# First step of an inference kernel rearranged: norm vectors transposed first, weight loads issued at once, first weight tile's products between the input transpositions

## The reference

```python
def rms_norm(x, g):
    xf = x.astype(jnp.float32)
    y = xf * lax.rsqrt(jnp.mean(xf * xf, axis=-1, keepdims=True) + EPS)
    return (y * g.astype(jnp.float32)).astype(x.dtype)

def half_step_ffn(x, g_pre, g_post, w_up, w_down):
    h = rms_norm(x, g_pre) @ w_up
    gate, up = h[..., :D_FF], h[..., D_FF:]
    y = (jax.nn.silu(gate) * up) @ w_down
    return x + 0.5 * rms_norm(y, g_post)
```

## Time and profile before

| | us |
|---|---|
| median of 3 runs | 1392.56 |
| lowest and highest | 1391.97, 1392.8 |
| span of the profiled execution, first to last instruction | 1389.6 |
| PE busy in it | 1266.4 (91%) |
| DVE, ACT, POOL busy | 936.1, 655.4, 290.0 |
| first weight product starts | 24.38 after the span's start |

### The profile page before, as it was taken

The page is one execution under the profiler, slowest core; times in us unless marked ns, Lnnn a source line. Parts: engine busy times, 40 slices in busy tenths (PEclk is TensorE's granted clock), DMA queues, the critical chain, the costliest instruction groups (busy, mean ns, idle before and its releaser), DMA issues.

```text
span 1389.6 us, 24055 instructions
## 1 busy us (share of the span) xinstructions
PE 1266.4 (91%) x9033; PEld 1202.5 (87%) x9033; DVE 936.1 (67%) x1555; ACT 655.4 (47%) x1100; POOL 290.0 (21%) x214
## 2 busy tenths in 40 slices
PE   5999999999367899999989999999966689999998
PEld 4999999889255899999989999987964479999998
DVE  3766644779996676664476665466999957766543
ACT  3544444444365654444455444454335475544432
POOL 3000000546461610000020000035564425000000
PEclk9999999999757999999999999999985599999998
DMA  5454555523200435454535455553340023545451
GB/s 173 141 184 159 164 173 164 161 92 125 87 0 1 161 122 181 151 165 156 165 119 184 154 171 164 164 190 122 106 138 1 0 70 123 173 160 180 144 167 58
DMA packets 179540, 184.63 MB, mean 133 GB/s; under 512 B 6627, under 2 KB 174827, under 8 KB 179470
## 3 DMA queue, kind: packets, MB, share of 16 engines
q1 hardware_dynamic: 178030, 181.93, 40.6%
q0 software_dynamic: 1056, 1.62, 0.5%
q10 hardware_dynamic: 384, 0.13, 0.0%
HBM read 179.73 MB, written 3.93 MB: 132 GB/s over the span
## 4 chain that ended last, share of the span: by engine, by line
PE 68%; DVE 25%; ACT 3%; issue 3%; DMA 0%; DVEq 0%; SPq 0%; ACTq 0%
PE ps L1110 21%; PE ps L1112 20%; PE ps L1111 20%; DVE yc L950 6%; DVE score L866 2%; DVE acc L736 2%; DVE m L864 2%; DVE x L757 2%; DVE hl L722 2%; DVE upd L749 1%; DVE prob L981 1%; DVE prob L969 1%; DVE ropb L839 1%; PE ps L1340 1%; DVE proj L843 1%
## 5 line engine op out<-in xcount | busy, mean ns | idle before, releaser
L1110 PE MATMUL ps<-hh,wlo 128*128 128x288 f32 x1920 | 575.8, 300 | 19.2 <-DVE hl L722 10.1
L1111 PE MATMUL ps<-hl,whi 128*128 128x288 f32 x1920 | 567.6, 296 | 0.0
L1112 PE MATMUL ps<-hh,whi 128*128 128x288 f32 x1920 | 565.8, 295 | 0.0
L712 DVE TENSOR_TENSOR wlo<-raw,whi 128x1024 fp32r<-128x1024 f32 (+1 forms) x269 | 320.5, 1193 | 287.0 <-ACT whi L403 283.7
L403 ACT ACTIVATE whi<-raw 128x1024 fp32r<-128x1024 f32 (+1 forms) x336 | 347.4, 1035 | 236.5 <-PE ps L1112 213.2
L1110 PEld LDWEIGHTS ps<-hh,wlo 128*128 128x128 f32 x1920 | 361.2, 188 | 27.5 <-issue 14.2
L1112 PEld LDWEIGHTS ps<-hh,whi 128*128 128x128 f32 x1920 | 362.7, 189 | 0.0
L1111 PEld LDWEIGHTS ps<-hl,whi 128*128 128x128 f32 x1920 | 361.9, 188 | 0.6
L1050 POOL TENSOR_TENSOR wlo<-raw,whi 128x1024 fp32r<-128x1024 f32 x67 | 166.3, 2499 | 492.1 <-ACT whi L403 492.0
L1110 PE MATMUL ps<-ghi,wlo 128*128 128x288 f32 x704 | 208.4, 296 | 0.0
L1111 PE MATMUL ps<-glo,whi 128*128 128x288 f32 x704 | 207.7, 295 | 0.0
(11 more groups left out here) (202 smaller groups left out, 1186.5 us busy)
## 6 DMA issues: line engine op xcount, KB each, us to landing
raw<-in_ffn_w_up SPq DMA_DIRECT2D x88, 1024.0 KB, 5.1
raw<-in_ffn_w_down SPq DMA_DIRECT2D x32, 1024.0 KB, 5.1
raw<-in_w_in SPq DMA_DIRECT2D x24, 1024.0 KB, 5.2
raw<-in_ffn_w_down SPq DMA_DIRECT2D x16, 768.0 KB, 4.5
raw<-in_w_out SPq DMA_DIRECT2D x8, 1024.0 KB, 5.1
kc<-in_cache_k SPq DMA_DIRECT2D x2, 1024.0 KB, 8.1
vc<-in_cache_v SPq DMA_DIRECT2D x2, 1024.0 KB, 8.3
xrow<-in_x_prompt SPq DMA_DIRECT2D x1, 1024.0 KB, 5.4
```

The costliest lines, as they stand in the source:

```text
L712: dve.tensor_tensor(wlo[:, split_slot, 0:n, :], raw[:, raw_slot, 0:n, cols], whi[:, split_slot, 0:n, :].bitcast(F32), ALU.subtract).then_i ...
L1110: pe.matmul(out, wlo[:, slot, k, :], hi, start=start, stop=False)
L1111: pe.matmul(out, whi[:, slot, k, :], lo, start=False, stop=False)
L1112: return pe.matmul(out, whi[:, slot, k, :], hi, start=False, stop=stop)
```

## The change

SP no longer waits for the identity before it issues the first two weight loads. PE waits for the identity and for the nine vector loads, transposes the vectors, and then waits for x. The first step of the first block has its own order, `very_first_step`: four slices of x are transposed; then, four times, the three products of tile 0 with slice k and the transpositions of slice k + 4; then tile 1 with slices 0 to 3, both tiles with slices 4 to 7, the taps' transpositions, and tiles 2 and 3, the sum of squares between them. ACT makes a whi after every second hh. DVE takes the copies and the low parts by turns, reads the low part's x from PSUM, and makes wlo of tiles 0, 2 and 3; POOL makes that of tile 1.

```diff
                     sp.dma_start(xrow[0:DEC, 2, :], ins["x_sample"][0]).then_inc(x_in, 16)
-                    sp.wait_ge(ident_in, 16)
                     sp.dma_start(raw[:, 0], strip_view("ffn1_w_up", 0, 0, D, 0)).then_inc(loaded[0], 16)
...
                 act.activation(hh[:, c, :], x[:, c, :], ACT.Copy, scale=par[:, c:c + 1]).then_inc(hh_ready, 1)
+                if c % 2:
+                    split_quad(0, 0, c // 2, old=False)
             act.wait_ge(ms_ready, 1)
-            for rel in range(4):
-                split_quad(0, 0, rel, old=False)
...
-            for c in range(KD):
+
+            def first_copy(c):
                 dve.wait_ge(x_T, c + 1)
                 dve.tensor_copy(x[:, c, :], bank(c % 4)).then_inc(x_ready, 1)
+
+            def first_low(c):
+                dve.wait_ge(hh_ready, c + 1)
+                dve.scalar_tensor_tensor(out=hl[:, c, :], in0=bank(c % 4), scalar=par[:, c:c + 1],
+                                         in1=hh[:, c, :].bitcast(F32), op0=ALU.mult, op1=ALU.subtract).then_inc(hl_ready, 1)
+
+            first_copy(0)
             dve.wait_ge(par_ready, 1)
-            dve.wait_ge(x_ready, KD)
-            for c in range(KD):
-                low_x(0, gain(0, 0, 0), c)
-            for rel in range(4):
-                split_quad(0, 0, rel)
+            for c in range(1, KD):
+                first_copy(c)
+                first_low(c - 1)
+                if c == 3:
+                    split_quad(0, 0, 0)
+            first_low(KD - 1)
+            dve.wait_ge(lo_ready, 2)
+            split_quad(0, 0, 2)
+            split_quad(0, 0, 3)
...
+            pool.wait_ge(lo_ready, 1)
+            split_lo(1, 0, 1, 1)
             sum_x(0)
...
+            def very_first_step():
+
+                def turn_x(c):
+                    if c >= 4:
+                        pe.wait_ge(hl_ready, c - 3)
+                    for tt, (t0, n) in enumerate(TOK):
+                        last = pe.transpose(bank(c % 4, lo=t0, n=n), xrow[0:n, tt, c * P:(c + 1) * P], ident[0:n, 0:n])
+                    last.then_inc(x_T, 1)
+
+                def part(rel, k):
+                    return triple(bank((4, 5, 7, 3)[rel]), rel, k, hh[:, k, :], hl[:, k, :], k == 0, k == KD - 1)
+
+                for c in range(4):
+                    turn_x(c)
+                for k in range(4):
+                    pe.wait_ge(hl_ready, k + 1)
+                    pe.wait_ge(lo_ready, 1)
+                    part(0, k)
+                    turn_x(k + 4)
+                pe.wait_ge(lo_ready, 2)
+                for k in range(4):
+                    part(1, k)
+                for k in range(4, KD):
+                    pe.wait_ge(hl_ready, k + 1)
+                    for rel in range(2):
+                        last = part(rel, k)
+                        if k == KD - 1:
+                            last.then_inc(w_used, 1)
+                pe.wait_ge(taps_in, 16)
+                for j in range(DEPTH * CT):
+                    last = pe.transpose(bank(1, lo=TAPS * j, n=TAPS), trow[:, j * P:(j + 1) * P],
+                                        ident[0:TAPS, 0:TAPS])
+                last.then_inc(taps_T, 1)
+                for rel in (2, 3):
+                    pe.wait_ge(lo_ready, rel + 1)
+                    for k in range(KD):
+                        last = part(rel, k)
+                    last.then_inc(w_used, 1)
+                    if rel == 2:
+                        pe.wait_ge(ms_ready, 1)
+                        sum_squares(0)
...
-                first_step(ffn_unit(f), hq, (4, 5, 7, 3), s=s)
+                if f == 0:
+                    very_first_step()
+                    pe.wait_ge(par_ready, 2)
+                else:
+                    first_step(ffn_unit(f), hq, (4, 5, 7, 3), s=s)
...
             pe.wait_ge(ident_in, 16)
-            pe.wait_ge(x_in, 32)
...
             pe.wait_ge(par_in, 16 * 9)
             pe.transpose(bank(6, n=120), prow[:], ident[0:120, 0:120]).then_inc(par_T, 1)
...
+            pe.wait_ge(x_in, 32)
```

## The result

| | us |
|---|---|
| before, median of 8 runs on the same chip | 1392.34 (1391.44 to 1393.49) |
| changed kernel, median of 8 runs | 1396.22 (1393.82 to 1396.93) |
| ratio, 95% interval | 1.0026 (1.0016 to 1.0036) |
| span of the profiled execution | 1391.9 (before 1389.6) |

What follows compares the result with a forecast made beforehand. TensorE, busy 91% of 1389.6 us, was taken as the bound, with the opening's chain deciding: first step ending at 42.1 instead of 39.5, +2.6 us, added to the 1392.56 median gives 1395.2, range 1391.0 to 1397.6.

Steps and rivals of the forecast that it cites:

- The number to beat: End of the first step in the kernel before, 39.5 us; everything later was said to be chained to it.
- First weight load at 18.2: Landing, 17.5 before: one DMA engine shared with the taps; bounds 0 and 1.3 us later, 0.7 later taken.
- Norm vectors at 11.8, free up to 15.1: TensorE starts when the vector loads land, near 11.8; no cost up to 15.1, then one us per us.
- From the load to the first product 3.4 us: Opening chain from first weight load to first product: 3.4 us, putting that product at 21.6 against 24.38.
- Four rounds, 6.3 us at the slow level: Three products plus one slice's transposition, four times, at 0.24 us a product: 6.3 us, to 27.9; 0.9 less if clock rises.
- TensorE at the sum of squares at 38.5: By its own order of rounds, remaining products, taps and third tile, TensorE reaches the sum of squares at 38.5 us.
- The sum ready at 38.5: Squares start at 29.9 and the sum's input is ready 8.6 us later, at 38.5, the moment TensorE gets there.
- so 8.6: First square to sum: 9.2 us before, less 0.6 of first-add excess, since GpSimd's first tensor operation is now another.
- End of the first step 42.1: Sum of squares at 38.5, plus 0.48 and 3.2 for the fourth tile's 24 products: 42.1, +2.6 us.
- the forecast's own case: The forecast's main case, chance 0.60: the change costs +2.6 us, spanning +0.7 to +3.9.
- A: Rival, chance 0.18: weights land early, first product at 18.3, everything 3.3 us earlier than forecast; likeliest 1391.
- B: Rival, chance 0.15: norm vectors wait behind the weight loads and land at 16.8; +4.3 us, 1396.9.

Runs made afterwards that it cites:

- e1: Kernel before with only SP's wait on the identity removed, so the weight loads issue at once; ratio 0.9994 to the kernel before.
- e4: Changed kernel with the taps loaded as 30 rows and 1 row instead of one load of 31; ratio 1.0002 to the kernel before.
- e10: Changed kernel plus 20 extra products in TensorE's wait for the weights, results overwritten; ratio 1.0034 to the kernel before.
- e5: Changed kernel with four slices of x transposed before the norm vectors instead of after; ratio 1.0018 to the kernel before.
- e12: Changed kernel plus 13 transpositions of the identity in TensorE's wait for the weights; ratio 1.0048 to the kernel before.
- e13_early_sum_filler: Changed kernel with squares early, low part 1 on VectorE, and 20 extra products in TensorE's wait for the weights; ratio 0.9991 to the kernel before.
- e3_no_mix: Changed kernel with all eight slices of x transposed before the first product, low parts reading x from SBUF; ratio 1.0017 to the kernel before.

## Why the prediction was right, point by point

- **The number to beat and what hangs on it.** Right up to 259 us: over all thirteen changed kernels the lag there is the end of the first step less 39.5, within 0.3 us. "Everything later is chained to it, with no clock time of its own" is wrong beyond: profiles with the opening of the kernel before (e1, e4, e10) are 3.0, 3.6 and 7.8 late at 1175. The medians of e1 and e4 don't follow; the profiled executions of e1 and e4 were slower than their medians by 1.5 and 1.3 us, and the change's was its fastest. The change's 3.6 us against an opening of 2.4 may hold 1 us of this, and the interval (2.2 to 5.0) can't tell.
- **First weight load at 18.2.** It landed at 16.7, and at 16.8 to 17.6 in the other kernels with the 31-row load. The step that failed is "I take 0.7" later: the bounds were no gain at all and 1.3 later, and the measured value lies outside them, 0.8 earlier (0.3 in e1). Over the ten kernels with the early issue it is 0.8 earlier to 0.1 later, so the bound of no gain and no loss was nearly right and the 0.7 was not there. That one DMA engine, the taps', sets the landing was right (e4).
- **Norm vectors at 11.8, free up to 15.1.** They landed by 11.4; free, as e5 shows.
- **From the load to the first product 3.4 us.** 3.3.
- **Four rounds, 6.3 us at the slow level.** 6.7: 1.65 to 1.69 each, the handover between a transposition and a product on top of 3 x 0.24 + 0.86. Pricing them at the lower clock was right (e10, e12).
- **TensorE at the sum of squares at 38.5.** By its own order it would have been there at 37.6; the early load took 1.5 off, the rounds put 0.4 back.
- **The sum ready at 38.5.** 38.0, and TensorE waited 0.60 us for it. The prediction had named a visible wait there as a sign that the squares and not the products set the end, and so they did, by this much. The squares started at 28.76 instead of 29.9, but "so 8.6" failed: 9.3, as before. The first add still took 1.61, though another GpSimd instruction had gone before. It ran beside VectorE's subtractions in SBUF (28.38 to 30.73); in e13_early_sum_filler the first add, with none beside it, took 0.80, and the last two, beside VectorE's two subtractions, took 2.73 together (rows below). The excess is the neighbour's, not the first instruction's.

```profile
16.19 0.80 POOL L1110 TENSOR_TENSOR accx<-accx,sq 128x288 f32<-128x288 f32 x1
...
27.38 2.73 POOL L1110 TENSOR_TENSOR accx<-accx,sq 128x288 f32<-128x288 f32 x2 [1.33 <-ACT sq L680]
...
26.49 2.96 DVE L736 TENSOR_TENSOR wlo<-raw,whi 128x1024 fp32r<-128x1024 f32 x2
```

- **End of the first step 42.1.** 41.9. The load, 1.5 too late in my sum, was nearly made up by rounds 0.4 and a sum of squares 0.7 too short: +2.6 predicted, +2.4 in the opening, 3.6 by the ratio. That the opening came within 0.2 us is thus in part luck, since errors of 1.5 and of 1.1 offset each other, and the median itself lies 1.0 above the forecast, which the interval cannot tell from none.
- **Rivals and chances.** A was out by the first high part at 16.75, B by the vectors at 11.4. In e4, where A's condition is made true, the prediction's -3.3 at the first product became -2.35 and the time a tie. The span of the forecast's own case, +0.7 to +3.9, is wider than its bounds make it: with the load at 17.5 and a fast clock +1.0, with the load 1.3 later +3.2. "Slower", by more than 0.2%, had a chance of 0.42, less than the 0.48 for no change that shows.

## What to carry to other kernels

Work put between the products of a tile cost the lower clock here as well as its own time: check at which of its two paces TensorE runs there. Before shortening a chain, find what ends second: here the product order and the sum of squares lay 0.6 us apart, so early squares alone gave 0.2 us of the opening, faster rounds alone 2.1 (they bring the last slice and its squares forward too), and both 4.6. And a small load can hold back a large one that is issued after it: the taps as 30 rows and 1 row instead of 31 gave 2.3 us of the opening here.

## What was not expected of the hardware

- VectorE's low part with both inputs in SBUF took 2.48 us beside a GpSimd subtraction, 0.51 otherwise; with x read from PSUM it took 0.51 beside one too.
- After the same wait for the sum (2.37 and 2.32 us) the granted clock fell in e3_no_mix (window 36 to 38 us, below) and not in e10_filler, whose products go on at 0.13.

```profile
36.00:38.00 2.00, 1.89 (x6) 1.63 (x7) 2.00 (x2) 1.98 (x2) 0.00 (x0) 0.50 0.00 0
```

- The time spent in the two mixer stages, whose work is the same in all fourteen kernels, moves by some 4 us each from profile to profile, with granted clocks of 0.72 to 0.79 there in those looked at, while the 440 us between them repeat to 0.2 us. A difference of 1 us in an opening needs a marker ahead of the first such stage; in the total it takes many runs. Why the times of e10 and e12, by their ratios, lie some 4 us above their openings and that of e13 about 1 is open.
